# Dilated scores of two head groups in one product of 128 rows, and token sums taken between the halves of a unit

## What is computed

```python
# first block, per layer
h = rms_norm(x, g_mix[l])
c_q, c_kv, k_r, qkv_b, qkv_c, gate_logits = split(h @ w_in[l])
y_a = mla_mixer(c_q, c_kv, k_r, ...)          # rms_norm of the latents c_q (256) and c_kv (128) inside
y_b = dilated_mixer(rope(q_b), rope(k_b), v_b)  # 12 heads of 64: 3 groups of 4
y_c = neighbourhood_mixer(...)
x = x + (gates . branches) @ w_o[l]
h = rms_norm(x, g_ffn[l])
x = x + (silu(h @ w1[l]) * (h @ w3[l])) @ w2[l]
# second block, per layer
h = layer_norm(x) * (1 + scale) + shift
q, k, v, g_a, cu, cb, cc, g_c, fu, g_f = split(h @ w_in_2[l])
y = concat(attention(...) * silu(g_a), cb * conv(cc * cu) * silu(g_c), fourier(fu) * silu(g_f))
x = layer_norm(ALPHA * x + (1 + gate) * (y @ w_out_2[l])) * ln_g + ln_b
```

## Time and profile before

| what | value |
|---|---|
| median of 3 executions | 2564.07 us |
| lowest and highest | 2562.38 and 2568.13 us |
| profiled execution, its own time | 2568.33 us |
| its span, first to last instruction | 2566.5 us |
| mean granted clock of TensorE | 0.989 of full |
| TensorE busy | 2493.5 us, 97% |
| POOL busy | 1938.6 us, 76% |
| VectorE busy | 1128.2 us, 44% |
| ScalarE busy | 669.2 us, 26% |

### The profile page before, as it was taken

How to read it: one execution, slowest core, us unless ns; L and a number is a source line. 1 busy time by engine, 2 the same in 40 slices (tenths; PEclk the granted TensorE clock), 3 DMA queues, 4 the chain that set the end, 5 groups by cost and what they waited for, 6 DMA issues and landing times.

```text
span 2566.5 us, 38041 instructions
## 1 busy us (share of the span) xinstructions
PE 2493.5 (97%) x12990; PEld 2002.1 (78%) x12990; DVE 1128.2 (44%) x1592; ACT 669.2 (26%) x1320; POOL 1938.6 (76%) x1567
## 2 busy tenths in 40 slices
PE   7999999999999999999999999999999999999998
PEld 6776777777888887777787777888887877778776
DVE  6557453224312125557634224422225338550765
ACT  4445232112201013435314111210002215231351
POOL 7788656899989889878764889998988574448704
PEclk9999999999999999999999999999999999999998
DMA  4233321223333323333421223333333121112301
GB/s 146 88 107 116 132 66 62 90 92 92 98 98 98 93 92 96 95 94 120 145 82 36 88 90 98 98 98 91 97 98 95 60 88 58 42 35 90 99 1 66
DMA packets 67569, 226.62 MB, mean 88 GB/s; under 512 B 7552, under 2 KB 16256, under 8 KB 66944
## 3 DMA queue, kind: packets, MB, share of 16 engines
q1 hardware_dynamic: 66016, 221.32, 27.4%
q10 hardware_dynamic: 1440, 3.79, 0.4%
HBM read 222.99 MB, written 2.10 MB: 88 GB/s over the span
## 4 chain that ended last, share of the span: by engine, by line
POOL 36%; PE 32%; issue 20%; DVE 5%; DMA 4%; POOLq 2%; ACT 0%; SPq 0%; DVEq 0%; ACTq 0%
POOL whi L477 18%; POOL wlo L480 12%; PE ps L575 8%; PE ps L577 8%; PE ps L576 8%; POOL raw L496 3%; POOL ada_acc L498 3%; DMA raw<-w_gate 2%; DMA raw<-w_abc 1%; PE ps L718 1%; PE ps L685 1%; DVE q_parts L1930 1%; POOLq L479 1%; PE ps L629 1%; PE ps L1133 1%
## 5 line engine op out<-in xcount | busy, mean ns | idle before, releaser
L477 POOL TENSOR_TENSOR whi<-raw,one 128x512 fp32r<-128x512 f32 (+3 forms) x732 | 793.4, 1084 | 505.0 <-PE ps L577 413.5
L480 POOL TENSOR_TENSOR wlo<-raw,whi 128x512 fp32r<-128x512 f32 (+3 forms) x732 | 955.7, 1306 | 57.4
L575 PE MATMUL ps<-h,whi 128*128 128x512 f32 (+1 forms) x1952 | 778.2, 399 | 27.3 <-POOL wlo L480 17.2
L576 PE MATMUL ps<-h,whi 128*128 128x512 f32 (+1 forms) x1952 | 764.6, 392 | 0.0
L577 PE MATMUL ps<-h,wlo 128*128 128x512 f32 (+1 forms) x1952 | 764.4, 392 | 0.0
L575 PEld LDWEIGHTS ps<-h,whi 128*128 128x128 f32 (+1 forms) x1952 | 368.1, 189 | 122.4 <-POOL wlo L480 30.0
L577 PEld LDWEIGHTS ps<-h,wlo 128*128 128x128 f32 (+1 forms) x1952 | 367.8, 188 | 79.1
L576 PEld LDWEIGHTS ps<-h,whi 128*128 128x128 f32 (+1 forms) x1952 | 368.4, 189 | 77.3 <-issue 2.4
L575 PE MATMUL ps<-y,whi 128*128 128x512 f32 x640 | 251.1, 392 | 0.6 <-DVE y L1852 0.6
L576 PE MATMUL ps<-y,whi 128*128 128x512 f32 x640 | 249.2, 389 | 0.0
L577 PE MATMUL ps<-y,wlo 128*128 128x512 f32 x640 | 249.2, 389 | 0.0
(11 more groups left out here) (290 smaller groups left out, 3059.7 us busy)
## 6 DMA issues: line engine op xcount, KB each, us to landing
raw<-w SPq DMA_DIRECT2D x120, 512.0 KB, 3.5
raw<-w_abc SPq DMA_DIRECT2D x68, 512.0 KB, 3.5
raw<-w_ada SPq DMA_DIRECT2D x48, 512.0 KB, 3.5
raw<-w_gate SPq DMA_DIRECT2D x48, 512.0 KB, 3.6
raw<-w_in SPq DMA_DIRECT2D x44, 512.0 KB, 3.5
raw<-w_pac SPq DMA_DIRECT2D x16, 512.0 KB, 3.5
raw<-w_o SPq DMA_DIRECT2D x16, 512.0 KB, 3.5
raw<-w_out SPq DMA_DIRECT2D x16, 512.0 KB, 3.5
```

The costliest lines, as they stand in the source:

```text
L477: pool.tensor_tensor(whi[:, s, r], raw[:, s, r], one[:, 0:1].to_broadcast([P, cols // 2]), ALU.mult).then_inc(hi_made, 1)
L480: pool.tensor_tensor(wlo[:, s, r], raw[:, s, r], whi[:, s, r].bitcast(F32), ALU.subtract).then_inc(made, 1)
L575: nc.tensor.matmul(out, whi[:, s, w], moving[:, c, :], start=(c == 0), stop=False)
L576: nc.tensor.matmul(out, whi[:, s, w], rest[:, c, :], start=False, stop=False)
```

## The change

It is one diff over all engines. Its core, with "..." where lines are left out:

```diff
+        out_g = at("out_g", [P, T], scr + 11 * TILE)
-        kb_ = at("kb", [P, B_TILES, T], hd + 6 * TILE)
+        kb_ = at("kb", [P, 2, T], hd + 6 * TILE)
+        kz = [at(f"kz{hh}", [P, NQB, 2, P], hd + o * TILE) for hh, o in enumerate((8, 10, 0, 6))]
...
# TensorE, start of a layer
-                unit(1, DC, h_hi, h_lo)
-                square_sums().then_inc(nsum_done, 1)
-                unit(0, DC, h_hi, h_lo)
-                spread_rs()
-                unit(1, DC, h_hi, h_lo)
+                unit(1, DC, h_hi, h_lo, halfway=lambda: square_sums().then_inc(nsum_done, 1))
+                unit(0, DC, h_hi, h_lo, halfway=spread_rs)
+                unit(1, DC, h_hi, h_lo, halfway=lambda: token_sums(sqa[0:1], last=False))
                 pairs(B_TILES - 1, DC, h_hi, h_lo)
-                unit(0, DC, h_hi, h_lo)
+                unit(0, DC, h_hi, h_lo, halfway=lambda: token_sums(sqa[1:2], first=False))
                 unit(1, DC, h_hi, h_lo, m=HD)
                 pe.wait_ge(rsb_ready, rb_n.next())
-                pe.wait_ge(bank_free[0], free_n[0].now() + 1)
-                token_sums(sqa[0:2])
-                token_sums(sqa[2:3], bank=7).then_inc(nsum_done, 1)
...
# TensorE, scores of groups 1 and 2 (q tile 2 + hh holds heads 4 + hh and 8 + hh)
-                            last = nc.tensor.matmul(ps[bank + 1][:, (g - 1) * P:g * P], q,
-                                                    kb_[r, hg // 2, ph * P:(ph + 1) * P], start=True, stop=True)
+                    return nc.tensor.matmul(ps[bank + 1][:, 0:2 * P], qb_[:, 2 + hh, q_rows],
+                                            kz[hh][:, ph].rearrange("p g i -> p (g i)"), start=True, stop=True)
...
# TensorE, first unit of the dilated values
-                unit(0, DC, h_hi, h_lo)
+                unit(0, DC, h_hi, h_lo, halfway=lambda: token_sums(sqa[2:3], bank=7).then_inc(nsum_done, 1))
...
# TensorE, feed-forward
-                        unit(0, DC, h_hi, h_lo, each=chunk_by_chunk(h_ready, h_n, DC))
-                        square_sums().then_inc(nsum_done, 1)
-                        unit(1, DC, h_hi, h_lo, halfway=spread_rs)
+                        unit(0, DC, h_hi, h_lo, each=chunk_by_chunk(h_ready, h_n, DC), bank=2)
+                        unit(1, DC, h_hi, h_lo, halfway=lambda: square_sums().then_inc(nsum_done, 1), bank=3)
+                        unit(0, DC, h_hi, h_lo, halfway=spread_rs)
+                        unit(1, DC, h_hi, h_lo)
...
# TensorE, block two
-                two_units(DC, h_hi, h_lo, chunk_by_chunk(h_ready, h_n, DC))
+                two_units(DC, h_hi, h_lo, chunk_by_chunk(h_ready, h_n, DC), (2, 3))
...
# VectorE, new
+                def b_keys_apart(hh):
+                    s = hh % 2
+                    dve.wait_ge(swapped[s], swap_n[s].next())
+                    nc.vector.tensor_tensor(tmp[s], ps[s][:], rope[:, 0, :], ALU.mult).then_inc(bank_free[s], 1)
+                    nc.vector.tensor_tensor(ps[4 + s][:], ps[4 + s][:], rope[:, 1, :], ALU.mult).then_inc(half_turned, 1)
+                    dve.wait_ge(bank_free[s], free_n[s].next())
+                    dve.wait_ge(half_turned, turned_n.next())
+                    for g in range(2):
+                        rows, others = slice(HD * g, HD * g + HD), slice(HD * (1 - g), HD * (1 - g) + HD)
+                        nc.vector.memset(kz[hh][others, :, g, :], 0.0)
+                        last = nc.vector.tensor_tensor(kz[hh][rows, :, g, :].rearrange("p f i -> p i f"),
+                                                       ps[4 + s][rows, :].rearrange("p (i f) -> p i f", f=4),
+                                                       tmp[s][rows, :].rearrange("p (i f) -> p i f", f=4), ALU.add)
+                    last.then_inc(fin_done, 1)
...
-                b_rope(kb_, 0, 2)
+                b_rope(kb_, 0, 1)
+                for hh in range(2):
+                    b_keys_apart(hh)
                 for hh in range(B_HEADS):
                     zero = HD * (1 - hh % 2)
                     nc.vector.memset(y[zero:zero + HD, B_KREST[hh], :].bitcast(F32), 0.0)
                 b_rest(kb_, B_K, lambda hh: (B_KREST[hh], hh % 2))
-                b_rope(kb_, 4, 1)
+                for hh in range(2, B_HEADS):
+                    b_keys_apart(hh)
...
# VectorE, end of residual_and_input: rest(6), rest(7), then square(6), square(7)
-                        if m >= 1:
+                        if 1 <= m < DC - 1:
                             rest_and_square(m - 1, gain)
-                    rest_and_square(DC - 1, gain)
+                    for m in (DC - 2, DC - 1):
+                        rest(m, gain)
+                    for m in (DC - 2, DC - 1):
+                        square(m)
...
# channel_parts goes from ScalarE to VectorE
-                        nc.scalar.activation(ac[:, blk, t].rearrange("p k c -> p (k c)"), ps[5 + 2 * (i % 2)][:, 0:2 * P],
-                                             ACT.Copy).then_inc(ch_used, 1)
+                        nc.vector.tensor_copy(ac[:, blk, t].rearrange("p k c -> p (k c)"),
+                                              ps[5 + 2 * (i % 2)][:, 0:2 * P]).then_inc(ch_used, 1)
...
# VectorE: the convolution's remainders move into the attention's loop
-                    put_y(t, conv_out[t])
+                def conv_rest(i):
+                    if i in (4, 8):
+                        put_y(i // 4 - 1, conv_out[i // 4 - 1])
```

More of the change, by code:

```diff
@@ L580, in tiles, with unit @@
                 return last
-            def unit(s, n, moving, rest, m=P, each=None, halfway=None):
-                pe.wait_ge(bank_free[s], free_n[s].next())
+            def unit(s, n, moving, rest, m=P, each=None, halfway=None, bank=None):
+                if bank is None:
+                    pe.wait_ge(bank_free[s], free_n[s].next())
                 split_n[s].next()
-                tiles(s, s, n, moving, rest, m, each=each, halfway=halfway).then_inc(unit_done[s], 1)
+                tiles(s if bank is None else bank, s, n, moving, rest, m, each=each, halfway=halfway).then_inc(unit_done[s], 1)
             def pairs(times, n, moving, rest, each=None):
@@ L596, in pairs, with two_units @@
                         unit(s, n, moving, rest)
-            def two_units(n, moving, rest, each):
+            def two_units(n, moving, rest, each, banks):
                 per = n // 2
                 for s in range(2):
-                    pe.wait_ge(bank_free[s], free_n[s].next())
                     split_n[s].next()
@@ L1062, in _ @@
                     head_sums(t - 2)
+                    if 2 <= t < 4:
+                        free_n[t % 2].next()
                 unit(0, DC, h_hi, h_lo)
@@ L1432, in _ @@
                 gate(7)
[L1434 to L1439 removed]
                 def g_out(qb, rest):
                     return (y[:, 8 * rest:8 * rest + 4, qb * P:(qb + 1) * P],
[L1443 to L1446 removed]
+                            out_g[:].rearrange("p (f q) -> p f q", q=P))
+                attention(8, T, lambda i: ps[2 + i % 3][:], False, g_out, ring_3, tmp, 5, gated=True)
                 for t in range(2):
@@ L1538, in attention @@
             def attention(n_heads, cols, maximum, move_pt, y_out, ring, slots, o_banks, out, r_bank, gated=False, between=None,
-                          group=2, behind=0, later=None):
+                          group=2, behind=0, later=None, aside=None):
                 n = NQB * n_heads
@@ L1855, in _ @@
+                for part, n in enumerate(FF_PARTS):
+                    peeled = 1 if part == 0 else 0
+                    if peeled:
+                        feed_forward(0, (2, 3))
+                    with repeat(dve, n - peeled, [(ud_n[0], 1), (ud_n[1], 1), (free_n[0], 1), (free_n[1], 1), (si_n, 1),
+                                                  (mhi_n, 1), (mg_n, 1)]) as j:
+                        feed_forward(j + peeled, (0, 1))
                     if part < 2:
@@ L2131 @@
     c_units = blocks(C_COL, 3 * C_TILES)
-    w_abc = np.concatenate([units(w_in, blocks(0, 2) + blocks(B_COL, 2 * B_TILES) + blocks(2 * P, 1)), kr_unit,
+    b_units = []
+    for first in (B_COL, B_COL + 12 * HD):
+        head = blocks(first, 12, HD)
+        b_units += blocks(first, 2) + [np.concatenate([head[4 + hh], head[8 + hh]]) for hh in range(B_HEADS)]
+    w_abc = np.concatenate([units(w_in, blocks(0, 2) + b_units + blocks(2 * P, 1)), kr_unit,
                             units(w_in, blocks(B_COL + 2 * B_TILES * P, B_TILES) + [c_units[i] for i in (8, 9, 10, 11, 0, 1, 4, 5, 2, 3, 6, 7)])], 1)
```

89 lines of the change are left out of this document (39 added, 50 removed).

## The result

The changed kernel takes 2569.84 us (median of 12 runs), the kernel before 2564.57 (12 runs on the same chip): a ratio of 1.0016, 95% interval [1.0009, 1.0024]. It is slower by 4 us by this ratio (5.3 by the medians), where I forecast 5 us less. The interval is clear of no change, but the loss is of the size that two groups of runs differ by: repeated on another chip, the same kernel gave 1.0003 (**after_again**). The profiled execution has a span of 2570.2 us, 3.7 more than that of before.

The account below looks back on a forecast made before the run. The prediction took TensorE, busy 97% of the span, as the bound, with idle time, small products and half clock to win or lose. Its terms summed to -5.3 us, from the median 2564.07 to 2558.8 us, range 2551 to 2566.

Parts of the forecast that it names:

- the wait for the sum: Layer 0 start: TensorE's wait for VectorE's input to the sum grows by half a unit, +2.7 us.
- the two new waits at the early spread: Layer starts: the spread, half a unit after unit 1, stalls 2.0 us for its input in each layer, +4.0 us.
- the feed-forward: Feed-forward's first two units: stalls for the last input chunk and the sum, and a clock fall, go: -6.6 us, both layers.
- the third unit: Block two's third unit: its 0.60 us wait for ScalarE goes, -1.4 us with the slower first product.
- the transforms: Channel transforms: VectorE's maxima come earlier, so TensorE's third transform and all behind it do too, -5.9 us with a clock fall.
- Two places, I take one fall, +1.5.: Layer starts: one clock fall behind the new stalls at the spread, +1.5 us (0 to 3).
- The fall behind the 24 should go, -3.3.: Latent sums: split into three groups of eight, they lose the clock fall behind them, 1.66 us a layer, -3.3 us.
- No stall, by half a microsecond.: Latents' spread: the root's chain takes about 2.2 us while the unit has 2.7 left, so TensorE doesn't wait.
- All 2.2 us come on top, +4.4.: Keys apart: VectorE's extra work on the fourth key tile lengthens TensorE's 1.33 us wait before the last latent unit, +4.4 us.
- 0.12 a step, -3.7.: Scores: two records of 128x256 replace four of 64x128, saving 0.12 us in each of 32 steps, -3.7 us.
- The rival by columns: Scores: a product is paid by its columns, so they give nothing, 2562.5 us; chance 10%.
- The slower rival: Small products between halves, seven places a layer, bring the clock down each time: +5 us, or 2575 us with all; chance 10%.

Follow-up runs that it names:

- start_back: Changed kernel with the layer-start sum again behind the whole second unit and the spread behind the whole third, as before: 2556.14 us, 0.9958 of before.
- sums_back: Changed kernel with the 24 latent-sum records in one place again, behind the 64-row unit: 2564.73 us, 0.9990 of before.
- no_product: Changed kernel without the 128-row score product of groups 1 and 2 in 14 of a layer's 16 dilated steps: 2567.77 us, 1.0008 of before.
- start_later: Changed kernel with the layer-start sum half through the third unit and the spread half through the fourth: 2555.02 us, 0.9954 of before.
- best2: Changed kernel, sum half through third unit, spread at its end, third latent-sum group half through 64-row unit, VectorE's key work reordered: 2543.64 us, 0.9920 of before.

## Why the prediction was wrong

The direction failed, and first of all by the step that priced what the waits at the layers' start bring behind them: one fall of the clock at 1.5 us, where the traces have 5.3 us of half clock. The terms that the forecast and the traces share are right in five places: the wait for the sum (+2.7 forecast, 4.25 - 1.55 = 2.7 found), the two new waits at the early spread (4.0; 2.54 + 1.50, though partly by luck: in after_again they are 2.54 and 2.75), the feed-forward (-6.6; -6.0), the third unit (-1.4; -1.6), the transforms (-5.9; -5.7). The steps that failed:

- **"Two places, I take one fall, +1.5."** They cost 5.3. I priced a fall at the 1.5 to 1.7 us of the earlier trace rows, though the wait ahead of it was to grow from 1.55 to 4.25, and the one fall then lasted 6.4 us instead of 3.3 (as long in six of the eight traces with this wait, half as long in two); and I doubted the fall behind the spread. This step alone turns the sum from a small gain towards none, and start_back shows the size of the part: 11.3 us less without it, against 8.2 forecast.
- **"The fall behind the 24 should go, -3.3."** It went, but in the changed kernel it would have been gone without the split: in sums_back no fall follows the 24 records. I took a fall for the property of the records in front of it.
- **"No stall, by half a microsecond."** 1.20 us in both layers, +2.4. The chain was priced at ten operations of 0.18 us. Two of them took 1.25 and 0.98 us, each to the end of an operation of POOL (last section), though the earlier trace rows already had one of 1.13 among four. VectorE, layer 0 of the changed kernel:

```profile
128.22 1.25 DVE L1682 TENSOR_TENSOR var<-var,rs 128x8 f32<-128x8 f32 x1
...
130.78 0.98 DVE L1686 TENSOR_TENSOR rs<-rs 128x8 f32<-128x8 f32 x1
```

- **"All 2.2 us come on top, +4.4."** 1.28 a layer. The fifth tile's read moved from 9.02 us behind the fourth's to 10.30; the four remainders took 3.14 instead of 3.84 us and gave some of it back. This was the one large error that made the forecast too slow; the fall behind it was right (+3.0; +3.3), in two executions of this same kernel three times out of four.
- **"0.12 a step, -3.7."** A dense step is 0.50 us shorter, not 0.20. But only the three steps ahead of the loop can use it in full, and behind the first two of them VectorE is late (transposes wait 0.27 us for it, and the unit before takes 5.82 instead of 5.58). The loop gives 0.5 us a layer, and no_product shows that a still shorter step gives nothing more; I had let near half of each step count. The rival by columns is refuted for these forms: 4 x 128 columns took 0.64 us and 2 x 256 took 0.24. The Trainium skill, "TensorE: Matmul & The Clock Gate", section "Back-to-back issue gap", gives for an isolated product the N/2.4 + 2.5 ns that I used, by which they would be equal but for 5 ns. The same section says that this under-counts small products in a stream, which the prediction left out. The rows agree with it: 0.64 us for the four, where the formula gives an estimated 0.22.

The misses add up: +3.8 for the layers' start, +2.4 for the new wait, -1.5 for the keys, +2.6 for the scores, 0.6 for the smaller terms, 7.9 us, from -5.3 to +2.6. The slower rival had the right side by the wrong mechanism. In start_later all seven small groups of a layer stand between halves, and the only falls of block one are behind its 2.61 us of wait at the keys; best2, with six of them between halves and the spread at a unit's end, has no fall there. The case that I should have priced is my own list of waits, with a fall of the clock behind each.

## What to carry to other kernels

Moving a small product into the middle of a dense stretch is free only if its input is there; compute when the producer delivers, at the slow duration of its small operations, and put the product half a unit later rather than half a unit earlier. In a kernel like this one, price a wait of TensorE over 2.5 us with a fall of its clock behind it, and one over 4 us with a fall that is mostly twice as long. Before work is moved into an engine's idle time, look on which side of the next needed operation that idle time lies, and look for a loop's floor before shortening its matmuls.

## What the runs showed of the hardware

**The clock falls behind waits, by chance that grows with the wait.** In the layers of block one (from 15 to 1960 us) of the 14 traces of this case, a window of 3 us with a granted clock below 0.92 stands at or within 3 us of 1 of 69 waits of 1.0 to 1.5 us, 5 of 41 from 1.5 to 2.0, 4 of 9 from 2.0 to 2.5, 22 of 29 from 2.5 to 2.9, and all 8 above 4; there is none between 2.9 and 4. In the 13 traces that have the change's feed-forward every fall there has a wait of over 1 us beside it. Only the kernel before has falls without one, four: behind the 24 records in each layer, and at the feed-forward's start in each, behind two waits below 1 us in a row.

**Small operations of VectorE end with POOL's.** VectorE and POOL at the spread of layer 0 in the changed kernel:

```profile
38.45 0.18 DVE L1471 RECIPROCAL rs<-std 128x4 f32<-128x4 f32 x1 [7.03 <-ACT std L1176]
38.66 0.98 DVE L1472 TENSOR_TENSOR nt<-rs 128x4 f32<-128x4 f32 x1
39.68 0.16 DVE L1473 SCALAR_TENSOR_TENSOR nt<-nt,var 128x4 f32<-128x4 f32 x1
39.87 1.11 DVE L1475 SCALAR_TENSOR_TENSOR rs<-nt,rs 128x4 f32<-128x4 f32 x1
```
```profile
38.58 1.04 POOL L479 TENSOR_TENSOR whi<-raw,one 128x512 fp32r<-128x512 f32 x1 [0.31 <-PE ps L579]
39.70 1.26 POOL L482 TENSOR_TENSOR wlo<-raw,whi 128x512 fp32r<-128x512 f32 x1
```

L1472 starts 0.08 us after POOL's L479 and ends at 39.64, POOL's at 39.62; L1475 starts 0.17 after L482 and ends at 40.98, POOL's at 40.96. L1473 starts in between and takes 0.16. The Trainium skill, "GPSIMD Engine Reference", section "Key points", says that the two engines share their SBUF interfaces and contend where VectorE has two SBUF inputs; the rows agree, and give the price: up to the rest of POOL's operation, here 1 us for four elements a partition. It also fits that the spread of layer 1 waited between 1.50 and 2.75 us in the eight traces with the changed kernel's start.
